# Products of zeros taken out of TensorE's queue in a two-layer trunk with a mixture of experts

## The reference

```python
g_logits = einsum('nd,dg->ng', xt, w_rg)                 # 4 groups
g_sel = argmax(g_logits)                                 # the best group
e_in_group = take(e_logits, g_sel)                       # its 8 experts
top_val, top_idx = lax.top_k(e_in_group, 2)              # the best two
top_w = softmax(top_val) * g_weight
...
hid = silu(xt @ w_gate[g]) * (xt @ w_up[g]) * combine    # 32 experts, width 256
out = out + hid @ w_down[g]
```

## Time and profile before

| | |
|---|---|
| Three runs | 601.21, 601.26, 606.39 us; median 601.26 |
| Profiled execution | 601.48 us, of which 599.8 us from the first to the last instruction |
| Mean granted clock of TensorE | 0.969 |
| Busy share | TensorE 90%, VectorE 30%, ScalarE 29%, GpSimd 1% |
| Chain that ended last, by engine | TensorE 62%, DMA 29%, VectorE 4%, ScalarE 3% |
| DMA | 236.14 MB, mean 394 GB/s |

### The profile page before, as it was taken

One profiled execution on the slowest core, in us unless ns is written; L12 is line 12 of the kernel. 1 busy time (PEld: TensorE's weight loads), 2 busy tenths in 40 slices (PEclk: granted clock), 3 DMA queues, 4 the chain that ended last, 5 costly groups with the idle time before them and its releaser, 6 DMA issues.

```text
span 599.8 us, 7996 instructions
## 1 busy us (share of the span) xinstructions
PE 536.9 (90%) x3338; PEld 297.6 (50%) x3338; DVE 182.1 (30%) x309; ACT 174.5 (29%) x309; POOL 6.5 (1%) x16
## 2 busy tenths in 40 slices
PE   5999899999999998768789999999999999987576
PEld 4888687444434433132268878874444244322211
DVE  3686944311111100010184466643111111101001
ACT  4845834021111111010285696540211111110101
POOL 0000000000000000000000000000000000000000
PEclk7999999999999999798799999999999999998998
DMA  8999999899999999999999974798999999999994
GB/s 306 424 420 419 421 420 423 314 425 420 419 422 419 421 421 420 421 417 418 422 419 421 421 325 146 266 424 311 425 421 421 420 420 421 421 420 421 418 419 198
DMA packets 33565, 236.14 MB, mean 394 GB/s; under 512 B 3760, under 2 KB 3760, under 8 KB 5488
## 3 DMA queue, kind: packets, MB, share of 16 engines
q1 hardware_dynamic: 32800, 232.07, 94.2%
q0 software_dynamic: 720, 3.45, 1.4%
HBM read 234.45 MB, written 1.05 MB: 393 GB/s over the span
## 4 chain that ended last, share of the span: by engine, by line
PE 62%; DMA 29%; DVE 4%; ACT 3%; SPq 1%; issue 1%; ACTq 0%; DVEq 0%
PE psum L1291 19%; DMA raw<-stream 18%; DMA late<-stream 9%; PE psum L262 8%; PE psum L263 8%; PE psum L264 7%; PE psum L1268 7%; PE psum L1339 6%; DMA xT<-x_turned 1%; SPq L209 1%; PE psum L519 1%; PE psum L1353 1%; PE psum L336 1%; ACT hid L1412 1%; PE psum L1118 1%
## 5 line engine op out<-in xcount | busy, mean ns | idle before, releaser
L1291 PE MATMUL psum<-raw,x 128*32 128x512 f32 x680 | 91.4, 638 | 25.7 <-DMA raw<-stream 14.5
L254 DVE TENSOR_TENSOR raw_lo<-raw,whi 128x1024 fp32r<-128x1024 f32 x52 | 62.4, 1221 | 45.1 <-ACT whi L247 44.9
L1339 PE MATMUL psum<-y,pickT 128*128 128x512 f32 x128 | 63.8, 620 | 4.5 <-ACT y L1418 3.5
L1268 PEld LDWEIGHTS psum<-pick,h 128*128 128x128 f32 x512 | 58.8, 192 | 18.2 <-issue 15.7
L247 ACT CAST whi<-raw 128x1024 fp32r<-128x1024 f32 x52 | 53.0, 1048 | 41.6 <-PE psum L264 35.3
L1268 PE MATMUL psum<-pick,h 128*128 128x128 f32 x512 | 63.0, 279 | 1.2 <-DVE pick L1235 1.0
L262 PE MATMUL psum<-whi,hnT_hi 128*128 128x512 f32 x144 | 57.8, 401 | 6.2 <-DVE hnT_lo L366 5.7
L1243 DVE TENSOR_TENSOR pick<-pick,lists 128x256 f32<-128x256 f32 x16 | 6.8, 424 | 175.7 <-PE psum L1353 175.7
L263 PE MATMUL psum<-whi,hnT_lo 128*128 128x512 f32 x144 | 57.7, 401 | 0.0
L264 PE MATMUL psum<-raw_lo,hnT_hi 128*128 128x512 f32 x144 | 57.1, 396 | 0.0
L1291 PEld LDWEIGHTS psum<-raw,x 128*32 128x32 f32 x680 | 18.3, 113 | 73.1 <-issue 45.8
(11 more groups left out here) (213 smaller groups left out, 497.2 us busy)
## 6 DMA issues: line engine op xcount, KB each, us to landing
raw<-stream SPq DMA_DIRECT2D x157, 1024.0 KB, 26.6
late<-stream SPq DMA_DIRECT2D x60, 1024.0 KB, 24.4
raw<-stream SPq DMA_DIRECT2D x2, 512.0 KB, 7.4
xT<-x_turned SPq DMA_DIRECT2D x2, 512.0 KB, 8.5
h<-x SPq DMA_DIRECT2D x1, 1024.0 KB, 12.5
pb<-even_bias POOLq DMA_DIRECT2D x1, 1024.0 KB, 13.9
pool_c<-even_pool POOLq DMA_DIRECT2D x1, 1024.0 KB, 9.4
pb<-even_bias POOLq DMA_DIRECT2D x1, 512.0 KB, 8.2
```

The costliest lines, as they stand in the source:

```text
L254: nc.vector.tensor_tensor(raw_lo[PLACE[c][0]][:, cols], chunk(c)[:, cols], whi[:, n % SPLIT, cols].bitcast(F32), ALU.subtract).then_inc(lo ...
L1268: mm = nc.tensor.matmul(psum[:, gather_banks(q)[part], kk * P:(kk + 1) * P], h[:, t, k * P:(k + 1) * P], pick[:, t, :], start=(t == 0), st ...
L1291: nc.tensor.matmul(psum[rows, b, :], lhs[:, rows], chunk(c)[:, e * W4:(e + 1) * W4], start=start, stop=stop).then_inc(moe_used, 1)
L1339: nc.tensor.matmul(bank(b), pickT[:, t * P:(t + 1) * P], y[:], start=(q == 0), stop=(q == QUADS - 1)).then_inc(m.scattered, 1)
```

## The change

All calls of `keep_warm_pe` go, the function too, GpSimd's filling of the tile, the semaphore, and the tile. TensorE's first instruction is now the wait for the constants. The tiles that were placed behind `zeros` lie 512 bytes lower in each partition. Nothing else is changed: no order of other instructions, and no wait between them.

```diff
-        zeros = fixed("zeros", [P, P], F32R)
...
-        zeros_ready = sem("zeros_ready")
-
-        def keep_warm_pe(n):
-            for _ in range(n):
-                nc.tensor.matmul(bank(3), zeros[:], zeros[:].unsqueeze(1).to_broadcast([P, 4, P]), start=True, stop=True, skip_group_check=True)
-
...
-            pe.wait_ge(zeros_ready, 1)
-            keep_warm_pe(12)
             pe.wait_ge(cst_landed, 16)
             even_block(0)
...
-            keep_warm_pe(2)
             pe.wait_ge(m.logitsT_ready, layer + 1)
...
             mm.then_inc(m.routed, 1)
-            keep_warm_pe(10)
...
                              skip_group_check=True).then_inc(m.ranked, 1)
-            keep_warm_pe(3)
...
-            nc.gpsimd.memset(zeros[:].bitcast(F32), 0.0).then_inc(zeros_ready, 1)
             even_pool_loads(pool)
```

## The result

The changed kernel took 608.09 us in the median of 15 runs (606.03 to 609.67); the kernel before, in 15 runs too, 601.26 us (598.13 to 606.39). The ratio is 1.0096 with a 95% interval of 1.0073 to 1.0120, a loss of 5.8 us (4.4 to 7.2). The forecast was 605.3 us, a loss of 4.0. The direction was right and the loss larger than the forecast. By its ratio the changed kernel stands at 607.0 us, inside of the range to 607.8; its own median is 0.3 us above that range, and the two medians lie 6.8 us apart. The profiled execution took 609.67 us with a span of 607.9 us, against 601.48 and 599.8 before; it is the longest of its 15, and shows more than the typical loss.

The account below looks back on a forecast made before the run. The weight stream, restarted in each layer once TensorE has used the experts' first chunk, was taken as the bound. The sum 601.48 + 0 + 0 + 2.0 + 2.0 = 605.5 us, 0.2 lower for the median, gave 605.3; range 601.0 to 607.8 us.

Parts of the forecast that it names:

- The bound: Experts of both layers: the weight stream restarts after the first chunk, and each microsecond of delay there moves the layer's end.
- The zeros delayed nothing: Routing: zeros hide behind VectorE's chain; removing them saves at most 0.4 us in both layers, taken as 0.
- The start: Kernel start: the lower clock lasts 3.46 us with or without the 12 zeros; taken as 0, bounds -0.3 to +1.6 us.
- The clock in the routing: Both routings: without zeros the clock falls before the first gather and stays low 4.5 us after dense work resumes.
- the rival that it holds: Both routings: the clock stays high up to the gather, so no cost, 601.3 us; chance 0.13.
- Its price: Ranking, first gather and first chunk at the lower clock: 2.0 us a layer, 4.0 us for both.
- That rival: End of layer 0's experts: the fall is avoided, giving back at most 3.2 us, 602.1 us; chance 0.12.
- The third rival, the late return: Start and both gathers: the clock comes back late, 6.87 us each, 608.9 us in sum; chance 0.15.

Follow-up runs that it names:

- ends_no_start: ends without the 12 products of zeros at the start; 598.89 us against 602.30 for the kernel before, ratio 0.9959.
- ends: Kernel before plus 15 products of zeros in sure holes of each layer's last group of experts; 598.85 us against 602.10, ratio 0.9940.
- no_route: Kernel before without the 2 + 10 + 3 products of zeros of each routing, the 12 at the start kept; 607.77 us against 601.37, ratio 1.0099.
- no_ten: Kernel before without the 10 products of zeros behind the turned logits in each routing; median 606.1 us against 601.37, ratio 1.0047.
- only_tail: Changed kernel plus 20 products of zeros spread through each layer's last group of experts; 603.11 us, ratio 1.0026 to the kernel before.
- only_ends: Changed kernel plus 15 products of zeros in sure holes of each layer's last group of experts; 603.12 us, ratio 1.0013 to the kernel before.
- no_start: Kernel before without the 12 products of zeros at the start, the routing's kept; 603.86 us against 601.37, ratio 1.0022.
- start30: Kernel before with 30 products of zeros at the start in place of 12; 601.32 us against 601.92, ratio 0.9986.
- only_ten: Kernel before with only the 10 products of zeros behind the turned logits kept in each routing; 604.26 us against 601.37, ratio 1.0041.
- ends_start: ends with 30 products of zeros at the start in place of 12; 602.07 us, ratio 1.0001 to the kernel before.
- tail_start: Kernel before with 30 products of zeros at the start and 20 spread through each layer's last group; 604.65 us, ratio 1.0048.

## Why the prediction was right in direction and too small in size

**The bound** was right. The stream restarts when TensorE has used up the experts' first chunk; its restart moved by 2.48 us and the piece of transfer at the layer's end by 1.86, so 0.6 us was won back in layer 0, which the prediction had ruled out; in layer 1 it was none (3.63 and 3.81 us). **The zeros delayed nothing**: right, the waits behind them are the same 0.06 us. **The start** at zero stands as far as the runs can tell: ends_no_start against ends gives 0.04 us by the medians. The 0.53 us that the profiled start lost is a longer stay at the lower clock (5.7 us from the first product at 10.95, against 3.46), and no_route, which has the 12 zeros, shows the like (its clock is back at 16.94).

**The clock in the routing** fell, in both layers, and the rival that it holds is out: the fall is in the profiles of after, no_route, no_ten, only_tail and only_ends, in both layers of each, and the first gathers there take 1.9 to 2.1 us. In the eight profiles with all zeros of the routing all 16 first gathers take 1.16 us. **Its price** was forecast as 2.0 us a layer, and the profiled pair shows 1.95 and 1.83. By the medians of ends and only_ends it is 4.3 us for both, against 4.0. That the size came out so near is in part luck, of two errors that offset each other. The stay behind the gather's start was 3.84 and 3.68 us, not 4.5, so gather and chunk lost 1.52 and 1.39 us, not 1.9; and the ranking, whose two pairs ran at the lower clock (0.69 and 0.58 us), lost 0.42 and 0.44 us where I had put 0.1. (With the factor 1.98 in place of 1.9 the term would be 4.2 us, not the 4.1 that the prediction gives.) The warning in the Trainium skill's page "TensorE: Matmul & The Clock Gate" (section "Why this matters for your kernels") is borne out by the two gathers at 2.09 us.

**What the sum left out is a cost at the layers' ends, which it took as they are.** The prediction named the clock there, as a gain only and only for layer 0. That rival did not come: in the changed kernel's profile the clock fell at 286.32 us, just as the awaited chunk was taken up (286.34), and stayed low for 6.83 us as before. In the profiled pair the last end cost 3.5 us, with a fall that lasted 13.66 us where it had lasted 3.42. The experiments show that the ends are a term of their own in both kernels: filling them won 3.25 us by the medians in the kernel before (602.10 to 598.85), and 5.0 us between the changed kernel (608.09) and only_ends (603.12), which were run at different times. That the two differ says the same as that the full change cost more (5.8 us) than the change with filled ends (4.3); it is no second evidence, and 4.3 lies just below the interval of 5.8 (4.4 to 7.2). Whether the changed kernel really falls into the bad case at its ends more often, or scatter makes up the missing 1.5 us, stays open. The low stretch at the last end was longer in no_start and start30, which keep the routing's zeros, than in no_route, no_ten and only_ten, so the 3.5 us of the profiled pair can't be put down to the change. The runs of the kernel before spread over up to 9 us, and no single profile of each settles it.

The third rival, the late return, had the right length (6.84 us at the lower clock in each routing), but counted it from the gather on; some 3 us of each stay lay ahead of the gather, where it cost little.

## What to carry to other kernels

Useless products in a hole of TensorE can be worth their place when the hole stands just ahead of work that restarts something larger, here a stream of weights, and no worth was found where the hole goes on behind them, as at the start. Put them only in holes that are there for certain, fewer than the hole holds (20 spread over each last group won nothing, 15 in its sure holes won 3.6 us), and look at every such hole on the path, the last microseconds too. When a kernel's runs scatter, look at the clock over several profiled executions before a change of a few microseconds is put down to the code.

## What the runs showed that I had not expected

The time of a fall is not tied to the program. The fall at the end of layer 0's experts came at 284.52 us before and at 300.56 in only_ten, and at the last end the clock was low for 3.42 us before, 10.2 in start30 and 13.66 in the changed kernel, for nearly the same work. The page named above says in its section "What's actually happening" that the point at which the clock rises at a kernel's start varies with the moment at which the first matmul lands. The traces agree that it varies (3.4 us behind the first real product in no_start, 5.9 in no_route), though by more than the 500 ns to either side that the page gives. They show the like for later falls and returns.

TensorE has a hole of 4 to 6 us at the first chunk of each layer's last group (5.60 us), for which the trace names no releaser. It stands where the code reads a flag and jumps over a block. In every profile the clock falls in it or within 0.6 us of its end (267.46 us before, 269.24 after). Its number is not the same in all kernels: with 18 more zeros at the start there is a second hole of 4.08 us in ends_start, and one of 4.64 in tail_start, but none in start30. What TensorE waits for in it, no run tested.
